# A hybrid decoder's mixers: half of the memory decays on ScalarE, the square root's table two steps earlier, and the sample memories' products in the inversion

## The reference

```python
x = ln(ALPHA * x + 0.5 * swiglu(x, ffn1))
p = x @ w_in
ya, shift, wkv = rwkv7(p[..., :RWKV_COLS], ...)
yb, conv, C, n, m = mlstm(p[..., RWKV_COLS:], ...)
x = ln(ALPHA * x + concat(ya, yb) @ w_out)
x = ln(ALPHA * x + 0.5 * swiglu(x, ffn2))
...
S = S * w_t + sa * (kk_t * a_t) + v_t * k_t      # rwkv7, per token; sa = S @ -kk_t, y = S @ r_t
...
C = dec * C + einsum('hs,hsd,hse->hde', ws, kc, vc)   # mlstm, per chunk of 64 tokens
h = (h - mean(h)) * rsqrt(var(h) + eps) * mh_g
```

## Time and profile before

| | |
|---|---|
| Median of 3 runs | 1521.6 us (1521.47 to 1523.23) |
| The profiled execution | 1519.59 us |
| its span | 1517.9 us |
| its mean granted TensorE clock | 0.986 |
| TensorE busy | 1464.3 us, 96% |
| VectorE busy | 985.0 us, 65% |
| ScalarE busy | 695.9 us, 46% |
| GpSimd busy | 378.2 us, 25% |

### The profile page before, as it was taken

How to read it: one execution, slowest core, us unless ns; L and a number is a source line. 1 busy time by engine, 2 the same in 40 slices (tenths; PEclk the granted TensorE clock), 3 DMA queues, 4 the chain that set the end, 5 groups by cost and what they waited for, 6 DMA issues and landing times.

```text
span 1517.9 us, 33992 instructions
## 1 busy us (share of the span) xinstructions
PE 1464.3 (96%) x13374; PEld 1409.3 (93%) x13374; DVE 985.0 (65%) x1579; ACT 695.9 (46%) x1188; POOL 378.2 (25%) x407
## 2 busy tenths in 40 slices
PE   7999999999989999999999999989999899999995
PEld 7999998899867999999999999979998689999995
DVE  4444435588476687775577776466865777877644
ACT  5333334765645543334443334366565465333332
POOL 4222363010532422220412222300115323222100
PEclk9999999999999999999999999999999999999998
DMA  8544543443214555444544545434521444555351
GB/s 221 150 144 149 168 149 88 126 128 101 55 34 134 157 160 151 146 141 150 159 137 142 151 152 156 152 88 123 129 78 33 123 121 136 165 150 167 126 166 35
DMA packets 318938, 198.82 MB, mean 131 GB/s; under 512 B 7792, under 2 KB 303760, under 8 KB 318832
## 3 DMA queue, kind: packets, MB, share of 16 engines
q1 hardware_dynamic: 315120, 190.69, 43.1%
q0 software_dynamic: 3712, 6.62, 2.1%
HBM read 188.50 MB, written 8.78 MB: 130 GB/s over the span
## 4 chain that ended last, share of the span: by engine, by line
PE 85%; DVE 7%; ACT 3%; issue 2%; DVEq 1%; DMA 0%; POOL 0%; SPq 0%; POOLq 0%; ACTq 0%
PE bank L2120 24%; PE bank L2122 23%; PE bank L2121 23%; DVE wlo L2613 2%; PE bank L2207 1%; DVE rlo L2644 1%; ACT whi L2410 1%; ACT z L1183 1%; PE bank L2212 1%; PE bank L764 1%; PE bank L752 1%; DVE raw L1578 1%; PE bank L2171 1%; PE bank L853 1%; PE bank L458 1%
## 5 line engine op out<-in xcount | busy, mean ns | idle before, releaser
L2410 ACT ACTIVATE whi<-raw 128x1024 fp32r<-128x1024 f32 x340 | 358.2, 1059 | 471.9 <-PE bank L2122 455.7
L2613 DVE TENSOR_TENSOR wlo<-raw,whi 128x1024 fp32r<-128x1024 f32 x340 | 421.2, 1243 | 230.1 <-ACT whi L2410 229.3
L2120 PE MATMUL bank<-rhi,whi 128*128 128x322 f32 x984 | 306.5, 311 | 0.0
L2122 PE MATMUL bank<-rhi,wlo 128*128 128x322 f32 x984 | 305.9, 311 | 0.0
L2121 PE MATMUL bank<-rlo,whi 128*128 128x322 f32 x984 | 304.8, 310 | 0.0
L2120 PE MATMUL bank<-xh,whi 128*128 128x320 f32 x912 | 286.2, 314 | 4.6 <-DVE xl L2787 3.5
L2121 PE MATMUL bank<-xl,whi 128*128 128x320 f32 x912 | 283.0, 310 | 0.0
L2122 PE MATMUL bank<-xh,wlo 128*128 128x320 f32 x912 | 282.9, 310 | 0.0
L2882 POOL TENSOR_TENSOR hl<-scratch,hh 128x320 f32 x88 | 146.9, 1669 | 495.4 <-DVE scratch L2734 379.7
L2120 PE MATMUL bank<-hh,whi 128*128 128x320 f32 (+1 forms) x704 | 218.4, 310 | 0.5 <-DVE wlo L2613 0.5
L2121 PE MATMUL bank<-hl,whi 128*128 128x320 f32 (+1 forms) x704 | 217.4, 309 | 0.0
(11 more groups left out here) (421 smaller groups left out, 1888.8 us busy)
## 6 DMA issues: line engine op xcount, KB each, us to landing
raw<-in_ffn_wg SPq DMA_DIRECT2D x88, 512.0 KB, 3.8
raw<-in_ffn_wu SPq DMA_DIRECT2D x88, 512.0 KB, 3.8
raw<-in_ffn_wd SPq DMA_DIRECT2D x88, 512.0 KB, 3.6
raw<-in_w_in SPq DMA_DIRECT2D x60, 512.0 KB, 3.8
raw<-in_w_out SPq DMA_DIRECT2D x16, 512.0 KB, 6.1
raw<-in_state_C SPq DMA_DIRECT2D x8, 512.0 KB, 6.1
out_s_C<-raw SPq DMA_DIRECT2D x8, 512.0 KB, 4.1
ring<-in_state_wkv POOLq DMA_DIRECT2D x8, 256.0 KB, 5.5
```

The costliest lines, as they stand in the source:

```text
L2120: pe.matmul(out, w_hi, hi, start=start, stop=False)
L2122: return pe.matmul(out, w_lo, hi, start=False, stop=stop)
L2410: act.activation(whi[:, slot, :], raw[:, slot, :], ACT.Copy).then_inc(hi_ready.sem, 1)
L2613: dve.tensor_tensor(wlo[:, slot, :], raw[:, slot, :], whi[:, slot, :].bitcast(F32), ALU.subtract).then_inc(lo_ready.sem, 1)
```

## The change

Three edits, all in the mixers, in both layers.

1. The pieces C1, C3, C5 and C7 (`DECAYED`) are scaled by ScalarE in place (`head_decay`, four operations of 128x128 each, at the steps 19 to 22, `DECAYS_AT`), and VectorE adds the bank to each piece in one operation of 128x512 instead of four that scale and add. The addition waits for the new signal `heads_decayed` besides `left_mm`.
2. The table set of the square root is loaded behind step 16's work instead of step 18's (`WEIGHTS_AT[2] + 2`).
3. The four sets of `samples_memory_products` move from the recurrence into the inversion's steps 25 and 26 (`OWN_AT`), two sets each, and write bank 7 instead of bank 3. ScalarE's copy of the sums (`s0sum`) moves from chunk 2 of the recurrence to chunk 0, the samples' r from chunk 2 to chunk 1, their u and its copies from chunk 3 to chunk 2; their y stays in chunk 3.

```diff
@@ -362,6 +362,7 @@
         h_ready = signal("h_ready", 2)
+        heads_decayed = signal("heads_decayed", 4)
         vmask_ready = signal("vmask_ready", HB // 2)
@@ -629,6 +630,7 @@
+        DECAYED = (1, 3, 5, 7)
         LEFT = (("C", 0), ("C", 1), ("C", 2), ("C", 3), ("H", 0), ("H", 1), ("C", 4), ("C", 5), ("C", 6), ("C", 7),
@@ -801,7 +803,7 @@
                 pe.wait_ge(side_copied.sem, side_copied.by(L, copied_by_scalar(NSIDE)))
-            sums = bank[3][:, :].rearrange("p (j s t) -> p j s t", j=NJ, s=2)
+            sums = bank[7][:, :].rearrange("p (j s t) -> p j s t", j=NJ, s=2)
             for b in range(SB):
@@ -868,11 +870,7 @@
                     last.then_inc(r_mm.sem, 1)
-                    if c == 1:
-                        samples_memory_products(pe, L, 1)
                     if c == 2:
-                        samples_memory_products(pe, L, 3)
-                    if c == 3:
                         samples_u(pe, L)
@@ -884,8 +882,6 @@
                 if c == 1:
-                    samples_memory_products(pe, L, 2)
-                if c == 2:
                     samples_r(pe, L)
@@ -904,8 +900,6 @@
                 last.then_inc(y_mm.sem, 1)
-                if c == 0:
-                    samples_memory_products(pe, L, 0)
@@ -963,12 +957,16 @@
                         left_over(pe, L, u)
+                if n in OWN_AT:
+                    for j in range(NJ // 2):
+                        samples_memory_products(pe, L, 2 * OWN_AT.index(n) + j)
             grow(pe, L, NSTEP - 1)
...
         HEAD_AT = (17, 18)
+        OWN_AT = (25, 26)
         LEFT_AT = (20, 20, 21, 21, 22, 22, 23, 23, 24, 24, 25, 26, NSTEP)
@@ -1138,6 +1136,15 @@
                            ACT.Square).then_inc(hsq_ready.sem, 1)
+
+        def head_decay(act, L, i):
+
+            h, half = 2 * (i // 4) + i % 2, i // 2 % 2
+            act.wait_ge(num_mm.sem, num_mm.by(L, NTT))
+            for s in range(4 * half, 4 * half + 4):
+                at = h * TS + s * ST + ST - 1
+                last = act.activation(C0[:, h, s, :], C0[:, h, s, :], ACT.Copy, scale=rexp[:, at:at + 1])
+            last.then_inc(heads_decayed.sem, 1)
@@ -1208,11 +1215,11 @@
             for c in range(NPC):
+                if c == 0:
+                    act.wait_ge(samples_mm.sem, samples_mm.by(L, 1))
+                    act.activation(s0sum[:, :, :, :].rearrange("p j s t -> p (j s t)"), bank[7][:, :],
+                                   ACT.Copy).then_inc(s0sum_ready.sem, 1)
                 if c == 2:
-                    act.wait_ge(samples_mm.sem, samples_mm.by(L, 1))
-                    act.activation(s0sum[:, :, :, :].rearrange("p j s t -> p (j s t)"), bank[3][:, :],
-                                   ACT.Copy).then_inc(s0sum_ready.sem, 1)
-                if c == 3:
                     act.wait_ge(samples_mm.sem, samples_mm.by(L, 3))
@@ -1271,16 +1278,19 @@
                     head_squares(act, L, SQUARES_AT.index(n))
-                if n == SQUARES_AT[0] + 1:
+                if n == WEIGHTS_AT[2] + 2:
                     act.preload_act_table_set("sqrt_and_others")
...
                     head_roots(act, L, ROOTS_AT.index(n))
+                if n in DECAYS_AT:
+                    head_decay(act, L, DECAYED[DECAYS_AT.index(n)])
             scalar_recurrence(act, L, split_hi)
...
         ROOTS_AT = (19, 22)
+        DECAYS_AT = (19, 20, 21, 22)
@@ -1572,7 +1582,11 @@
                 h, half = 2 * (i // 4) + i % 2, i // 2 % 2
-                for k in range(4):
+                if i in DECAYED:
+                    own = C0[:, h, 4 * half:4 * half + 4, :].rearrange("p b e -> p (b e)")
+                    dve.wait_ge(heads_decayed.sem, heads_decayed.by(L, DECAYED.index(i) + 1))
+                    last = dve.tensor_tensor(own, own, b[:, :], ALU.add)
+                for k in range(0 if i in DECAYED else 4):
                     s = 4 * half + k
@@ -1629,7 +1643,7 @@
                     tt(rsb[:, :, :], heads4(bank[0]), yr[:, slot(c), :, :], ALU.add).then_inc(r_ready.sem, 1)
-                if c == 3:
+                if c == 2:
                     dve.wait_ge(samples_mm.sem, samples_mm.by(L, 3))
@@ -1657,7 +1671,7 @@
                     dve.drain()
-                if c == 2:
+                if c == 1:
                     dve.wait_ge(samples_mm.sem, samples_mm.by(L, 2))
```

## The result

The change makes the kernel slower: 1527.2 us (1525.54 to 1528.16, 10 runs) against 1522.33 us (1518.31 to 1526.37, 10 runs) before. The ratio is 1.0029, with an interval of 1.0018 to 1.0041, so some 4.4 us. Forecast were 1519.4 us, 1514.5 to 1525.0; the time lies above the range.

A forecast was written before the change was run, and what follows sets the result against it. TensorE was taken to bound the kernel, busy 96% of the span. Layer 0: 1.59 - 0.85 - 1.73 = -0.99; layer 1: 1.59 - 0.85 - 1.97 = -1.23; together -2.2 from 1521.6 us gives 1519.4 us, range 1514.5 to 1525.0.

The forecast's parts named there:

- the clock: Half speed of TensorE in the mixers: no gain or loss counted; in the tail up to 1.7 us a layer.
- the rivals: Three other outcomes: holes stay, 1523.1 us (0.23); products hide, 1512.1 us (0.17); the tail starves too, 1526.6 us (0.14).
- the row of half speed behind 450: Sign of a wrong forecast: TensorE granted half speed after 450 us in layer 0's timeline.
- The slower rival: TensorE also runs out of instructions in the inversion's tail: +2.50 us per layer, 1526.6 us, chance 0.14.
- The first u: Start of the recurrence behind the inversion's tail: -2.06 + 3.65 = +1.59 us in each layer.
- The relief ahead of the tail: Before the inversion's tail, per layer: 0.77 table load, 0.80 decayed pieces, 0.28 and 0.21 small waits, 2.06 us.
- the base: One profiled execution, 1519.59 us, 2.0 below the median of 1521.6; the difference of -2.2 was set against the median.
- Table load: ScalarE's 1.28 us load in the inversion hides in idle time at step 16, saving 0.77 us per layer.
- Decays: Decayed pieces: VectorE saves 0.40 us each, 0.80 per layer counted; ScalarE pays 1.1 us each in idle time.
- Products: 128 matmuls of 64x16 per layer in steps 25 and 26 cost 0.0285 us each, 3.65 us in a full tail.
- the rival: Products run beside the inversion's own products and in waits for masks, costing nothing: 1512.1 us, chance 0.17.
- Recurrence and holes: Recurrence without products: -0.85 us per layer; TensorE's waits for instructions there vanish: -1.73 in layer 0, -1.97 in layer 1.

The follow-up runs named there:

- before's first profile: The unchanged kernel, the profiled execution on which the prediction rests; it took 1519.59 us.
- Before's second profile: The unchanged kernel run and profiled again; 1523.77 us beside 1523.67, ratio 0.9994.
- the kernel with the table alone: The kernel before with only the table set's load moved to step 16; 1522.55 us, ratio 0.9997.
- table and decays: The kernel before with the table load's move and ScalarE's decays, products left in the recurrence; 1521.35 us, ratio 0.9990.
- the kernel where half speed stayed away until then: Table and decays, plus five 384-column matmuls per layer where TensorE waits for VectorE; 1521.82 us, ratio 1.0000 to the kernel before.
- the kernel with wide matmuls: The whole change plus eight 256-column matmuls per layer between the products, read by nobody; 1533.53 us, ratio 1.0089 to the kernel before.

## Why the prediction was wrong

**The step that failed is the clock.** The working took 1.00 for the whole tail and recurrence, counted "neither gain nor loss" for half speed, and gave 1.7 us a layer as what a stretch of it in the tail would cost, with no chance and no place in the sum. The change has 10.2 us of it from the tail into the recurrence in both layers. In layer 0, by its rows, the second block takes 1.4 us more than 64 passes at the first block's pace (58 in 1.80), the last grow step 0.4 more than at full speed, and the recurrence 1.6 more than 15.72: 3.4 us, and for two layers, by estimate, 6.8 of the 7.45 between the two profiled executions. None of the rivals was this one; of the signs of being wrong, the row of half speed behind 450 is the one that came. The slower rival came out near in time, 1526.6, by luck: its mechanism, TensorE without instructions in the tail, is nowhere, and no hole is left in tail or recurrence.

The first u shows the same. It was to come 1.59 us later and comes 6.4 and 5.0 us later than in before's first profile. The relief ahead of the tail, -2.06, isn't there: the transposes at the tail's start (L458, now L459) begin 1.5 us later in layer 0, behind the half speed from 442.0 to 448.8, and at the same place in layer 1. From them to the first u it takes 4.9 and 5.0 us more, where 3.65 was forecast.

**The second failure is the base.** One execution was taken for the kernel. Before's second profile has mixers that are 4.4 and 6.0 us longer, mostly from half speed. A sum of terms of 0.2 to 1 us can't be tested against such a base, unless it says what the clock does.

The other steps:

- Table load: hidden, right. From the load to the VectorE addition that waits for the numerators' copy (L1530, now L1540), and so free of what lies ahead, the change and the kernel with the table alone agree (8.90 us in layer 0); the latter reached that addition 0.8 and 0.7 us earlier after the inversion's head than before's first profile, against 0.77 forecast.
- Decays: 0.43 saved per piece, right, 1.26 us on ScalarE for 1.1. But the relief of 2.06 ahead of the tail never reached the first u: table and decays brought it forward by 0.8 and 1.0 us, and 1.6 and 1.0 in the kernel where half speed stayed away until then. VectorE's gain ended in waits for TensorE at half speed.
- Products: 58 passes in 1.80 us are 0.031 each where 0.0285 was forecast, so in blocks of 64 they don't hide, and the rival falls for this order. But the prediction's reason, that interleaved passes were no faster than one after the other, reads the rows wrongly. The passes start in pairs 6 or 7 ns apart (by the program's order, one on each half of the partitions), and a pair every 58 ns, so the price holds two side by side already. Where before's inversion issues its two grow products by turns, four passes start in each 58 ns:

```profile
433.57 0.23 PE L764 MATMUL bank<-spare,z 64*64 64x64 f32 x2
433.59 0.23 PE L767 MATMUL bank<-z,spare 64*64 64x64 f32 x2
433.63 0.23 PE L764 MATMUL bank<-spare,z 64*64 64x64 f32 x2
433.65 0.22 PE L767 MATMUL bank<-z,spare 64*64 64x64 f32 x2
```

  The Trainium skill, TensorEngine Tiling (Array Packing), section Tiling Modes, has tiles work independently; the trace agrees for these. At the end of the change's first block the last six passes overlap the next product in the same way, and their records begin out of the order written. Products issued by turns with the inversion's own, in the quarters that these leave free, were not run, so whether they would hide is open.
- Recurrence and holes: right. Forecast were 18.50 - 0.85 - 1.73 = 15.92 us from the first u to the first memory without holes; at full speed it is 15.72, twice.
- At full speed, then, the change is about even: the kernel with wide matmuls, less their 5.9 us, has its first memory at 85.5 and 86.6 us, before's first profile at 86.7 and 86.1. That is, by estimate from one execution of each, 0.7 us less in all where -2.2 was forecast; the 4.4 is then the clock's.

## What to carry to other kernels

Before work is moved into a stretch bound by TensorE, look at the granted clock of that stretch in more than one profile, and ask whether what is added leaves TensorE with a long run of small passes: the price of a pass can double, for it and for what follows at half speed (a pair of passes every 107 ns for 58). A small set of such passes can go into a wait that ends on another engine; one that just fits (0.91 us in 0.86) gained 5.4 us here by itself, where the three edits of the change lost 4.4. When runs of one kernel spread by more than the effect that is sought, a single profile is one draw, and the mean clock over the runs tells which.

## What the runs showed of the hardware

In the change, half speed followed a stretch in which TensorE's records leave no gap. The Trainium skill, TensorE: Matmul & The Clock Gate, section What's actually happening, says that the clock is held back by default and released by activity. By that a TensorE without a gap would be expected to keep its speed, and the trace differs: busy for 10.2 of 10.2 us at 1.00, then 0.51, with products of 16 columns as the last work. Why it fell stays open.

The holes are TensorE's instructions coming late: they stood where some 230 matmuls and their weight loads had to run while the loads of `w_out` filled the DMA engines, each ended 1.3 to 1.6 us after an instruction packet had landed, and they are absent in all eight recurrences that have 256 TensorE instructions fewer and in six of the other twenty. The Trainium skill, Runtime: NRT & Kernel Launch, section Instruction fetch mechanics, calls the crossing of a block mostly hidden; here it cost 1.2 to 2.9 us where it showed (fourteen recurrences).

A matmul of 256 columns in this number format, run as two passes, took 0.63 us in the chain between products of 64x64, and one of 384 columns 0.68 (five in a row in 3.42).
